# Gate and up of a SwiGLU layer as one matrix product in seven block products instead of eight (Strassen, Winograd's form), with partial sums kept in PSUM

## The reference, cut to what matters

```python
def layer(x, ...):
    ...
    x = x + merged @ w_out
    h2 = rmsnorm(x, g_ffn)
    x = x + (jax.nn.silu(h2 @ w_gate) * (h2 @ w_up)) @ w_down
    return x, new_pool, v

def reference(...):
    ...
    y_prompt = rmsnorm(xp, g_final)
    y_sample = rmsnorm(xs, g_final)
```

## Time and profile before

| what | value |
|---|---|
| median of 3 runs | 822.46 us (822.36 to 823.38) |
| the profiled execution, its own time | 822.43 us |
| its span, first to last instruction, slowest core (core 1) | 820.9 us |
| spans of the eight cores | 819.4 to 820.9 us |
| granted TensorE clock, mean of each core | 0.995 to 0.997 |
| busy: PE, DVE, ACT, POOL | 98%, 43%, 26%, 13% of the span |
| longest stretches of the chain that ended last | PE, 94% of the span |

### The profile page before, as it was taken

One profiled execution on the slowest core, in us unless ns is written; L12 is line 12 of the kernel. 1 busy time (PEld: TensorE's weight loads), 2 busy tenths in 40 slices (PEclk: granted clock), 3 DMA queues, 4 the chain that ended last, 5 costly groups with the idle time before them and its releaser, 6 DMA issues.

```text
span 820.9 us, 12941 instructions; the slowest of 8 cores (819.4 to 820.9 us)
## 1 busy us (share of the span) xinstructions
PE 807.3 (98%) x4672; PEld 429.4 (52%) x4672; DVE 355.8 (43%) x582; ACT 212.1 (26%) x422; POOL 108.8 (13%) x193
## 2 busy tenths in 40 slices
PE   8999999999999999999999999999999999999996
PEld 4544545555555554455554455555544555555443
DVE  3699774444444457732124522122243212212776
ACT  4595443222222223321110011211100121121333
POOL 4153310000000012120100020101000210100211
PEclk9999999999999999999999999999999999999999
DMA  9974645121212164566311053222300451320233
GB/s 183 230 232 80 79 70 86 26 40 26 39 27 39 26 103 67 78 116 103 52 26 26 1 78 52 36 41 29 50 1 1 66 89 27 49 29 2 106 154 154
DMA packets 47584, 55.84 MB, mean 68 GB/s; under 512 B 28065, under 2 KB 28577, under 8 KB 47506
## 3 DMA queue, kind: packets, MB, share of 16 engines
q0 software_dynamic: 15840, 28.84, 23.9%
q1 hardware_dynamic: 31246, 25.86, 11.9%
q10 hardware_dynamic: 436, 0.31, 0.2%
HBM read 68.93 MB, written 9.01 MB: 95 GB/s over the span
## 4 chain that ended last, share of the span: by engine, by line
PE 94%; issue 2%; ACT 1%; DMA 1%; DVE 1%; POOL 0%; POOLq 0%; ACTq 0%; DVEq 0%
PE ps L450 91%; DMA ring<-wpk 1%; PE ps L1031 1%; ACT junk L471 1%; PE ps L870 1%; POOL rs L598 0%; PE ps L732 0%; ACT Fb L471 0%; PE ps L626 0%; PE ps L886 0%; DVE mrg L486 0%; ACT hT L471 0%; DVE hT L497 0%; POOL ring L505 0%; DVE actr L486 0%
## 5 line engine op out<-in xcount | busy, mean ns | idle before, releaser
L450 PE MATMUL ps<-hT,ring 128*128 128x416 f16 (+5 forms) x2704 | 473.7, 334 | 1.9 <-ACT hT L471 1.0
L450 PEld LDWEIGHTS ps<-hT,ring 128*128 128x128 f16 x2704 | 258.4, 98 | 206.2 <-issue 3.5
L471 ACT ACTIVATE Fb<-ps 128x416 f32<-128x416 f32 (+4 forms) x228 | 117.4, 519 | 484.0 <-PE ps L450 385.1
L481 DVE TENSOR_TENSOR actr<-Fb,ps 128x416 f16<-128x416 f32 (+2 forms) x126 | 75.0, 597 | 241.3 <-PE ps L450 237.4
L450 PE MATMUL ps<-ring,actr 128*128 128x512 f16 (+1 forms) x712 | 153.1, 377 | 0.0
L505 POOL DMA_DIRECT2D ring<-wpk x107 | 57.0, 546 | 456.6 <-PE ps L450 443.5
L481 DVE TENSOR_TENSOR X<-X,ps 128x512 f32<-128x512 f32 (+2 forms) x133 | 88.8, 680 | 64.9 <-PE ps L450 64.6
L450 PEld LDWEIGHTS ps<-ring,actr 128*128 128x128 f16 x712 | 69.4, 98 | 81.3
L481 DVE TENSOR_TENSOR Fb<-Fb,ps 128x416 f32<-128x416 f32 (+1 forms) x80 | 46.8, 585 | 93.4 <-PE ps L450 89.1
L471 ACT ACTIVATE junk<-X 128x1025 f16<-128x1025 f32 (+4 forms) x53 | 54.5, 1029 | 84.5 <-DVE X L481 81.4
L598 POOL TENSOR_TENSOR rs<-ss,mhalf 128x1 f32<-128x1 f32 (+1 forms) x67 | 48.5, 724 | 172.3 <-ACT junk L471 171.0
(11 more groups left out here) (76 smaller groups left out, 209.9 us busy)
## 6 DMA issues: line engine op xcount, KB each, us to landing
ring<-wpk POOLq DMA_DIRECT2D x107, 256.0 KB, 5.7
X<-xp SPq DMA_DIRECT2D x16, 512.0 KB, 8.3
yp<-mrg SPq DMA_DIRECT2D x15, 512.0 KB, 2.6
mrg<-cst SPq DMA_DIRECT2D x2, 512.0 KB, 7.2
mrg<-cst SPq DMA_DIRECT2D x2, 256.0 KB, 9.3
hb<-wpk POOLq DMA_DIRECT2D x2, 256.0 KB, 4.4
actr<-cst SPq DMA_DIRECT2D x1, 512.0 KB, 7.0
nps<-st SPq DMA_DIRECT2D x1, 448.0 KB, 9.7
```

What stands on the lines that cost most here:

```text
L450: ins = e.matmul(out=ap, lhsT=l, rhs=rr, start=(start and i == 0), stop=(stop and i == len(pairs) - 1))
L471: return e.activation(out=P.r(out), in_=P.r(in_), func=func, scale=scale, **kw)
L481: return P.add(eng, lambda e: e.tensor_tensor(out=P.r(out), in0=P.r(a), in1=P.r(b), op=op), reads=[a, b], writes=[out], dur=vdur(n, 1.04), ...
```

## The change

Gate and up of one f are taken as one product: two blocks of output channels (gate, up) by two halves of the channels K (512 each) times two halves of K by two halves of the tokens (`HALF` = 1032). Eight block products become seven. The token halves are cut into three column blocks of `HB` = 344, so that a unit of work, called a quad, is one f with 344 tokens of the first half (c1) and 344 of the second (c2). There are 22 x 3 = 66 quads. With g1, g2, u1, u2 for the K halves of the gate and up weights of f and H(r,c) for K half r and token half c of `hT`:

- token sums, once for all f (`half_sums`, three times 4 DVE operations of 4 x 344 elements): h1 = H(0,c2) - H(0,c1), h2 = H(1,c2) - h1, h4 = H(1,c1) - h2, and H(0,c2) is replaced by H(1,c2) - H(0,c2)
- weight sums, once per f (`weight_sums`, 4 DVE operations of 512 elements): s1 = u1 + u2, s2 = s1 - g1, s4 = g2 - s2, and u1 is replaced by g1 - u1
- products of 4 matmuls of 344 columns: p1 = g1 H(0,c1), p2 = g2 H(1,c1), p6 = s2 h2, p5 = s1 h1, p7 = (g1-u1)(H(1,c2)-H(0,c2)), p4 = u2 h4, p3 = s4 H(1,c2)

Bank `pa` takes p1, p6, p7 and p4 one after the other, `pd` takes p5 and p3, `pb` takes p2. ACT copies `pa` out after p1 (into r1), after p6 (r2) and after p7 (r3), each time before PE may add the next product. DVE adds `pb` to r1 (gate of c1), `pd` after p5 to r3 (up of c2), `pd` after p3 to r2 (gate of c2), and makes the two products with Silu. So a quad has 28 matmuls, 5 ACT operations and 5 DVE operations.

The results now lie in `actf` (the memory of `merged`), the token sums in `actr`; other buffers move with them (`gffn`, `gfin`, `ybuf`, `samT`). The tiles of the output projection run in the order 0, 8, 1, 9, NT, 2, 10, 3, 11, ... so that both token halves come forward together, and three times a set of token sums is put in (after tiles 10, 13 and 15). In the first group the quads of the first two f run as (0,0), (0,1), (1,0), (1,1), (0,2), (1,2), written (place of f in the group, column block).

```diff
-GRAN = 32
+HALF = TOK // 2
+HB = HALF // 3
+GRAN = 16
...
-        gffn = actr[:, 7, 0:2048].bitcast(F32)
+        gffn = actr[:, 6, 0:2048].bitcast(F32)
...
+        actf = merged
+        hsum = actr[:, 0:6, :].rearrange("p a t -> p (a t)").rearrange("p (s k t) -> p s k t", s=3, k=4)
+        wsum = [actr[:, 7, 0:1536].rearrange("p (s c) -> p s c", s=3),
+                hb[:, :, :].rearrange("p a c -> p (a c)")[:, 0:1536].rearrange("p (s c) -> p s c", s=3)]
+        wsum.append(actf[:, 7, 0:1536].rearrange("p (s c) -> p s c", s=3))
+        qbuf = [Fb[:, :, :].rearrange("p a c -> p (a c)")[:, i * HB:(i + 1) * HB] for i in range(6)]
+        qbuf.append(wsbs[:, 0:2 * HB].bitcast(F32))
...
-        for t in [0, 1, 2, 3, NT] + list(range(4, NT)):
+        def half_sums(j, prio):
+
+            q = [hT[:, 4 * r:4 * r + 4, c * HALF + j * HB:c * HALF + j * HB + HB] for (r, c) in
+                 ((0, 0), (0, 1), (1, 0), (1, 1))]
+            h1, h2, h4 = (hsum[:, i, :, j * HB:j * HB + HB] for i in range(3))
+            for (o_, x, y) in ((h1, q[1], q[0]), (h2, q[3], h1), (h4, q[2], h2), (q[1], q[3], q[1])):
+                vtt(o_, x, y, ALU.subtract, prio, 4 * HB, per=0.52)
+
+        order3 = []
+        for t in range(8):
+            order3 += [t, t + 8]
+            if t == 1:
+                order3.append(NT)
+        for n_, t in enumerate(order3):
...
             h_last = norm(t, gffn, pr + 1.0)
+            if t in (10, 13, 15):
+                half_sums((10, 13, 15).index(t), pr + 25.0)
...
+        def weight_sums(f, prio):
+            g1, g2 = U(('wg', f))[:, 0:512], U(('wg', f))[:, 512:1024]
+            u1, u2 = U(('wu', f))[:, 0:512], U(('wu', f))[:, 512:1024]
+            s1, s2, s4 = (wsum[2 if f == 1 else f % 2][:, i, :] for i in range(3))
+            for (o_, x, y, op) in ((s1, u1, u2, ALU.add), (s2, s1, g1, ALU.subtract), (s4, g2, s2, ALU.subtract),
+                                   (u1, g1, u1, ALU.subtract)):
+                vtt(o_, x, y, op, prio, 512, per=0.52)
+
+        def quad(f, fl, j, prio):
+
+            c1, c2 = j * HB, HALF + j * HB
+            q = len(quads)
+            pa, pb, pd = PT(), PT(), PT()
...
+            r1 = qbuf[(0, 1, 6)[q % 3]]
+            r2, r3 = qbuf[2 + q % 2], qbuf[4 + q % 2]
+            aft = [quads[q - 1]['p5'], quads[q - 2]['p7']] if q > 1 else []
...
+            prod('p1', pa, W(g[:, 0:512]), H(0, c1), True, aft)
+            act(r1, PV(pa, sl), AF.Copy, prio)
+            prod('p2', pb, W(g[:, 512:1024]), H(1, c1), True)
+            vtt(r1, r1, PV(pb, sl), ALU.add, prio, HB)
+            act(r1, r1, AF.Silu, prio)
+            prod('p6', pa, W(ws_[:, 1, :]), S(1), False)
+            act(r2, PV(pa, sl), AF.Copy, prio)
+            prod('p5', pd, W(ws_[:, 0, :]), S(0), True)
+            prod('p7', pa, W(u[:, 0:512]), H(0, c2), False)
+            act(r3, PV(pa, sl), AF.Copy, prio)
+            vtt(r3, r3, PV(pd, sl), ALU.add, prio, HB)
+            prod('p4', pa, W(u[:, 512:1024]), S(2), False)
+            prod('p3', pd, W(ws_[:, 2, :]), H(1, c2), False)
+            vtt(actf[:, fl, c1:c1 + HB], r1, PV(pa, sl), ALU.mult, prio, HB)
+            vtt(r2, r2, PV(pd, sl), ALU.add, prio, HB)
+            act(r2, r2, AF.Silu, prio)
+            vtt(actf[:, fl, c2:c2 + HB], r2, r3, ALU.mult, prio, HB)
+            quads.append(m)
...
-                for bi, (c0, W) in enumerate(BLK):
...
-                    mm(pG, sl, [(U(('wg', f))[:, k * 128:(k + 1) * 128], hT[:, k, c0:c0 + W]) for k in range(8)], pr)
...
-                    act(Fb[:, fi, :W], PV(pG, sl), AF.Silu, pr)
-                    mm(pU, sl, [(U(('wu', f))[:, k * 128:(k + 1) * 128], hT[:, k, c0:c0 + W]) for k in range(8)], pr)
-                    vtt(actr[:, fl, c0:c0 + W], Fb[:, fi, :W], PV(pU, sl), ALU.mult, pr, W)
...
+            todo = [(fl, j) for fl in range(nf) for j in range(3)]
+            if gi == 0:
+                todo[0:6] = [(0, 0), (0, 1), (1, 0), (1, 1), (0, 2), (1, 2)]
```

More of the change, by code:

```diff
@@ L439, in pt_, with mm @@
             return PT()
-        def mm(pt, sl, pairs, prio, start=True, stop=True):
+        def mm(pt, sl, pairs, prio, start=True, stop=True, after=(), skip=False):
             out = PV(pt, sl)
@@ L450, in fn @@
                     ins = e.matmul(out=ap, lhsT=l, rhs=rr, start=(start and i == 0),
-                                   stop=(stop and i == len(pairs) - 1))
+                                   stop=(stop and i == len(pairs) - 1), skip_group_check=skip)
                 return ins
@@ L454, in mm @@
             per = max(25.0, n / 2.4 * f + 2.5)
-            return P.add('pe', fn, reads=rd, writes=[out], dur=per * len(pairs), lat=220.0, prio=prio)
+            return P.add('pe', fn, reads=rd, writes=[out], dur=per * len(pairs), lat=220.0, prio=prio, after=after)
         def pe_multi(pt, items, prio, per, reads, nmm):
@@ L478, in vdur, with vtt @@
             return n * per + 70.0
-        def vtt(out, a, b, op, prio, n, eng='dve'):
+        def vtt(out, a, b, op, prio, n, eng='dve', per=1.04, after=()):
             return P.add(eng, lambda e: e.tensor_tensor(out=P.r(out), in0=P.r(a), in1=P.r(b), op=op),
-                         reads=[a, b], writes=[out], dur=vdur(n, 1.04), lat=200.0, prio=prio)
+                         reads=[a, b], writes=[out], dur=vdur(n, per), lat=200.0, prio=prio, after=after)
         def vstt(out, a, sc, b, op0, op1, prio, n):
@@ L926, in final_tile @@
                 mm(pt, lambda p, n=n: p[:, :n],
-                   [(actr[:, i, t * 128:(t + 1) * 128], U(('wd', f0 + i))[:, c0:c0 + n]) for i in range(nf)], pr)
+                   [(actf[:, i, t * 128:(t + 1) * 128], U(('wd', f0 + i))[:, c0:c0 + n]) for i in range(nf)], pr)
                 xv = X[:, t, c0:c0 + n]
@@ new lines, in build_nc, with prod @@
+        quads = []
+        def quad(f, fl, j, prio):
+            c1, c2 = j * HB, HALF + j * HB
+            q = len(quads)
+            pa, pb, pd = PT(), PT(), PT()
+            sl = lambda p: p[:, :HB]
+            W = lambda ap: [ap[:, k * 128:(k + 1) * 128] for k in range(4)]
+            g, u, ws_ = U(('wg', f)), U(('wu', f)), wsum[2 if f == 1 else f % 2]
+            H = lambda r, c: [hT[:, 4 * r + k, c:c + HB] for k in range(4)]
+            S = lambda i: [hsum[:, i, k, c1:c1 + HB] for k in range(4)]
+            r1 = qbuf[(0, 1, 6)[q % 3]]
+            r2, r3 = qbuf[2 + q % 2], qbuf[4 + q % 2]
+            aft = [quads[q - 1]['p5'], quads[q - 2]['p7']] if q > 1 else []
+            m = {}
+            def prod(nm, pt, w, x, first, after=()):
+                m[nm] = mm(pt, sl, list(zip(w, x)), prio, start=first, skip=True, after=after)
+            prod('p1', pa, W(g[:, 0:512]), H(0, c1), True, aft)
[16 more added lines that the diff above has]
+            quads.append(m)
@@ L979, in build_nc @@
             pv = sample_fm(lambda i, dd: U(('wd', f0 + i))[:, dd * 128:(dd + 1) * 128],
-                           lambda i: actr[:, i, SEQ:TOK], nf, base + 200.0)
+                           lambda i: actf[:, i, SEQ:TOK], nf, base + 200.0)
             if gi == 0:
```

35 lines of the change are left out of this document (17 added, 18 removed).

## The result

| | before | changed |
|---|---|---|
| median of 4 executions, us | 822.41 (822.21 to 823.38) | 793.43 (792.09 to 793.91) |
| ratio, 95% interval | | 0.9643 (0.9626 to 0.9659) |
| profiled execution: span of the slowest core, us | 820.9 | 791.7 |
| spans of the other cores, us | 819.4 to 820.2 | 785.3 to 790.1 |
| PE's waits, border and first quads, slowest core, us | 0 | 6.3 |

The kernel is faster by 29.0 us; 35.4 were forecast (787.1, range 784.0 to 801.0).

A forecast was written before the change was run, and what follows sets the result against it. PE was taken to bound the kernel by its column count. From 822.43 us, 38.0 net of PE's matmul time came off, 2.2 for the border and 0.5 for group starts and ends were added: 787.1, range 784.0 to 801.0.

The forecast's parts named there:

- the likeliest case: Whole kernel: 787.1 us, from 784.4 with no waits to 793 with a dear border; chance 0.72.
- steady waits: Rival: PE waits regularly in gate and up, for late weight sums or narrowly missed spares; 794 to 804 us, chance 0.17.
- Columns to time: Gate and up on PE: 344-column matmuls at 145.6 ns each, 4.08 us a quad, 269.1 us for all quads.
- No waits in the steady run: Gate and up: all spares positive but small, so no steady wait charged; 0.5 us for starts and ends of groups.
- The price of the copy's crossing: Gate and up: from a product's end on PE through ACT's copy back to PE, 0.26 + 0.455 + 0.14 = 0.86 us.
- the spare of 0.05 us for DVE's row: Gate and up: DVE's chain from p3 of one quad to the next takes 2.87 us against five products, 2.91.
- Price of the weight sums: DVE in gate and up: 512 f16 elements at 420 ns, the lower bound; 685 ns the upper.
- The border: Output projection to feed-forward layer: p7 begins 5.9 us after T, PE's end of that projection; PE waits 1.8, with 0.4 added.
- Keeping the add at T+1.85: Border to the feed-forward layer: DVE's last add to X still ends 1.85 us after the output projection ends on PE (T).
- Weights for the third f ... they are early: Feed-forward layer's start: loaded after the last transpose as before, needed by PE 24.5 us after the output projection's end (T).
- The rival in which the clock falls in gate and up: Part of gate and up at 1.2 GHz, needing steady waits first; a third of them would give 877 us; chance 0.03.
- Moves at no cost: Outside gate and up: new tile order, sums beside the output projection, moved buffers and an unchanged final stage add nothing.

The follow-up runs named there:

- e11: Changed kernel with second token sums, third and fourth f's sums and final gain later, quads reordered, Silu table early, gain load split, first weight sums later: 787.19 us.
- e9: Changed kernel with a quad's first product only after the last two products of the quad before, so quads no longer interleave: 913.87 us, ratio 1.1124.
- e6: Changed kernel with the final gain's 512 KB load sent with the feed-forward layer's second group, not right behind the last transpose: 791.67 us.

## Why the prediction held, and where it was off

- **The time as a whole.** It fell into the range, but not for the reason the range was made so wide. 793.4 lies just above the likeliest case (784.4 to 793), in the part kept for steady waits, and there were none. The 6.3 us over the forecast come from a late core, which no rival named. Of e11's 787.2, too, no more should be made than it is: another kernel, with fewer waits and a longer end than the sum for 787.1.
- **Columns to time.** Held: 146.0 ns measured, 145.6 forecast; 0.7 us over all quads.
- **No waits in the steady run.** Held on every core. The price of the copy's crossing held too (0.86 in e9). But the spare of 0.05 us for DVE's row was wrong as a size: whole durations were added, where following operations start 0.42 and 0.34 us apart, and the places of the weight sums were taken as fixed. With twice and four times the sums PE still didn't wait beyond 0.4 us in all. The rival "some steady waits" was given 0.17 for a danger that wasn't near.
- **Price of the weight sums.** Held at the lower bound, 420 ns.
- **The border.** Right in mechanism and, on the early cores, in size: adds at T+2.5 for T+1.85, 1.9 us of waits for 1.8, and a span of 785.3 where the sum gives 785.6. That the span is met to 0.3 us is in part chance: on core 1 the columns took 0.7 more, all charged waits 0.5 less, the end after PE's last matmul 1.2 more, and T came 1.7 earlier than in the earlier trace rows. The step that failed is "Keeping the add at T+1.85 (DVE has a set of token sums there as well, but two normalisations stand behind the adds in exchange)". On the late cores it came at T+3.9 to T+5.4: up to 2.8 us later than on core 1. The kernel before hid DVE's lateness in slack that the new sums use up, and the profile of before showed it, on core 1 itself; the prediction looked at that core's border and not at how late DVE had been on its way there.
- **"Weights for the third f ... they are early".** Right for PE and wrong for DVE. The new sums read the weights earlier than PE does, and in DVE's row even the fourth f's stood ahead: 2.2 us on the slowest core. A load had been checked against its old reader only.
- **One core for eight.** The sum was made for one core, and the time is the latest of eight. In each of the changed kernel's four executions the cores' spans part by 5.5 us or more.
- **The clock.** The rival in which the clock falls in gate and up didn't come. But "It needs steady waits first" isn't borne out: behind a single stop of 2.4 us on core 0 and of 3.4 us on core 2 the clock was lower for a few us (0.79 and 0.86 in the windows above), at some 1.5 us each, for which the sum had nothing. In e9, which idles in every quad, it was 1.00. The Trainium skill's section "A second HAM failure mode: psum-queue depth-cycling" ("TensorE: Matmul & The Clock Gate") tells of a kernel whose brief idling between groups made the clock swing; e9's rows show no such swing.
- **Moves at no cost.** Nearly: after PE's last matmul the changed kernel takes 8.1 to 8.5 us, the one before 7.3 to 7.6. No run looked at why.

What stays open: whether e6's later load saves anything of the fourth f's stop, why one core of a pair gets its loads later, and the last 1.1 us of waits for DVE in e11.

## What to carry to other kernels

When a change gives a second engine work, the question isn't only whether it has the time on average: ask what that slack was absorbing, in the profile of every core, and price the latest one. Where an in-order engine gets an operation that waits for a load, check the load against that operation, not against the old reader; and keep it behind whatever the bound engine wants sooner. Partial sums that go back and forth between engines cost nothing as long as two chains are interleaved (0 against 2.04 us a quad here).
